# One score pair to a step: regrouping the scores of an attention stage

## The reference

```python
def block(args):
    qi, i = args
    s = jnp.einsum('bqhmd,bkhmd->bhmqk', qi, kf)
    q_chunk = (i * Q_BLOCK + jnp.arange(Q_BLOCK)) // CHUNK
    mask = k_chunk[None, :] <= q_chunk[:, None]
    p = jax.nn.softmax(jnp.where(mask, s, -1e30), axis=-1)
    a = p[:, :, 0] - lam * p[:, :, 1]
    return jnp.einsum('bhqk,bkhe->bqhe', a, vf)
...
ga, gb, gc = jnp.split(jax.nn.sigmoid(h @ gate_w[l] + gate_b[l]), N_BRANCHES, axis=-1)
```

## Time and profile before

| | before |
|---|---|
| median of 3 runs | 3073.64 us (3070.15 to 3075.08) |
| the profiled execution: its time, its span | 3070.15 us, 3068.3 us |
| TensorE busy over the span | 2786.3 us, 91% |
| VectorE busy | 1984.3 us, 65% |
| ScalarE busy | 1462.1 us, 48% |
| attention stage, from and to | 511 to 1166 us of the span |

### The profile page before, as it was taken

One profiled execution on the slowest core, in us unless ns is written; L12 is line 12 of the kernel. 1 busy time (PEld: TensorE's weight loads), 2 busy tenths in 40 slices (PEclk: granted clock), 3 DMA queues, 4 the chain that ended last, 5 costly groups with the idle time before them and its releaser, 6 DMA issues. The chain is left out here.

```text
span 3068.3 us, 41252 instructions
## 1 busy us (share of the span) xinstructions
PE 2786.3 (91%) x13492; PEld 2197.5 (72%) x13493; DVE 1984.3 (65%) x3104; ACT 1462.1 (48%) x2353; POOL 388.4 (13%) x289
## 2 busy tenths in 40 slices
PE   4999887989999997899996898995999999999996
PEld 3767665777777775788874677884777777777774
DVE  6657995555545465544453564437888888888874
ACT  4414553555556463323343333212666666666663
POOL 3101221000000001101110001110122222222211
PEclk9999999999999998989997999997999999999998
DMA  6275325131322226311127997533989997877875
GB/s 229 92 261 198 96 83 149 57 117 59 97 83 80 78 78 238 96 42 52 49 76 249 307 314 263 198 139 139 367 269 308 355 369 246 284 234 219 264 256 144
DMA packets 292202, 554.80 MB, mean 181 GB/s; under 512 B 32089, under 2 KB 98905, under 8 KB 288482
## 3 DMA queue, kind: packets, MB, share of 16 engines
q1 hardware_dynamic: 273666, 492.06, 46.3%
q0 software_dynamic: 14400, 52.44, 7.0%
q10 hardware_dynamic: 4000, 8.53, 0.9%
HBM read 418.21 MB, written 143.15 MB: 183 GB/s over the span
## 5 line engine op out<-in xcount | busy, mean ns | idle before, releaser
L2596 DVE TENSOR_TENSOR moe_w_lo<-moe_W,moe_w_hi 128x1024 fp32r<-128x1024 f32 x384 | 461.0, 1221 | 85.5 <-ACT moe_w_hi L2524 72.1
L2524 ACT CAST moe_w_hi<-moe_W 128x1024 fp32r (+1 forms) x384 | 401.3, 1052 | 152.2 <-PE moe_h1b L2447 77.1
L1562 PE MATMUL project_bank<-h_lo,w_hi 128*128 128x512 f32 x512 | 201.7, 394 | 0.0
L340 PE MATMUL att_bank<-h_hi,w_hi 128*128 128x512 f32 x384 | 169.6, 442 | 17.0 <-PEq L137 11.6
L2472 PE MATMUL moe_yb<-moe_W,moe_hT 128*128 x384 | 172.5, 592 | 0.0
L519 DVE TENSOR_SCALAR_CACHE_REDUCE att_S<-att_bank 128x512 f32<-128x512 f32 x192 | 122.3, 687 | 63.5 <-PE att_bank L307 63.5
L2445 PE MATMUL moe_h1b<-moe_w_hi,moe_xT_hi 128*128 128x512 f32 x384 | 156.4, 407 | 4.8 <-DVE moe_xT_lo L2607 4.8
L425 ACT ACTIVATE att_S<-att_S,att_nm 128x128 f32<-128x128 f32 (+15 forms) x128 | 154.0, 1205 | 7.5 <-DVE att_nm L527 7.5
L341 PE MATMUL att_bank<-h_lo,w_hi 128*128 128x512 f32 x384 | 152.0, 396 | 0.0
L342 PE MATMUL att_bank<-h_hi,w_lo 128*128 128x512 f32 x384 | 152.0, 396 | 0.0
L2447 PE MATMUL moe_h1b<-moe_w_hi,moe_xT_lo 128*128 128x512 f32 x384 | 151.7, 395 | 0.0
(11 more groups left out here) (478 smaller groups left out, 6929.8 us busy)
## 6 DMA issues: line engine op xcount, KB each, us to landing
moe_W<-in_moe_w SPq DMA_DIRECT2D x96, 2048.0 KB, 13.4
w_raw<-in_gate_w SPq DMA_DIRECT2D x48, 512.0 KB, 3.9
out_sg<-gateT SPq DMA_DIRECT2D x32, 768.0 KB, 11.1
gateT<-att_gates SPq DMA_DIRECT2D x48, 256.0 KB, 2.3
gateT<-gate_out SPq DMA_DIRECT2D x48, 256.0 KB, 2.4
early<-in_ada_w SPq DMA_DIRECT2D x8, 1024.0 KB, 9.3
project_spare<-in_x SPq DMA_DIRECT2D x16, 512.0 KB, 6.2
w_raw<-in_w_in SPq DMA_DIRECT2D x16, 512.0 KB, 4.4
```

What stands on the lines that cost most here:

```text
L340: pe.matmul(bank[7][:], w_hi[b][:, k, :], h_hi[:, k, at], start=k == 0, stop=False)
L1562: pe.matmul(bank[n % 4][:], w_hi[b][:, k, :], low[:, k, at512(tb)], start=False, stop=False)
L2524: nc.scalar.copy(w_hi[:, slot(p, first), :], raw(at, p)).then_inc(q["w13_high"], 1)
L2596: nc.vector.tensor_tensor(w_lo[:, own, :], raw(at, p), w_hi[:, own, :].bitcast(F32), ALU.subtract).then_inc(q["w1_low" if p < 4 else "w3_l ...
```

## The change

TensorE makes the scores of `ahead` spread over the steps that are left, rounding up: with 1 to 4 pairs and 2 to 5 steps this is one pair in each step from step 0 on, until they are used up. VectorE evacuates three quarters of `ahead`, rounded up, ahead of the scales and the weighing: 1, 2, 3 and 3 pairs of 1, 2, 3 and 4, where it was 1, 2, 2 and 2. For three pairs (tiles 6 to 9) none is left behind the weighing, for four (tiles 10 to 13) one. The number of instructions and their sizes stay.

```diff
-    def scored_in(step, ahead):
-
-        return ahead[step:step + 2] if step % 2 == 0 else []
...
-                            for p in scored_in(n - lo, ahead):
-                                score(h, p)
+                            for _ in range(-(-len(ahead) // (hi + 1 - n))):
+                                score(h, ahead.pop(0))
...
-                        for p in ahead[:2]:
+                        most = -(-len(ahead) * 3 // 4)
+                        for p in ahead[:most]:
                             evacuate(h, p)
                         scales(item + 1)
                         weigh(item + 1)
-                        for p in ahead[2:]:
+                        for p in ahead[most:]:
                             evacuate(h, p)
```

## The result

The changed kernel takes 3109.07 us (median of 4 runs, 3101.39 to 3116.32), the kernel before 3074.36 (4 runs). The ratio is 1.0102, with a 95% interval of 1.0084 to 1.012: slower by 1.0%. Over all 22 runs on record the changed kernel's median is 3106.73 us (3098.35 to 3116.32). The prediction was 3105 us, slower. The profiled execution took 3104.89 us with a span of 3103.1, 34.8 us more than before.

What follows compares the result with a forecast made beforehand. TensorE was taken to bound the attention stage. Group costs and later weighings, less vanished stalls, summed to 8.07 us a head, 32.3 in four, giving 3102.5 or 3106 us, stated as 3105; range 3084 to 3119.

Steps and rivals of the forecast that it cites:

- TensorE sets the pace: Attention stage, 655 us long: TensorE busy in 610.53 us, so added TensorE work and its waits count.
- a group costs s = 0.37 us: TensorE, each group of score matmuls: 0.37 us at its edges; 16 more groups a head, 5.9 us.
- the two halves I read: Edges of a score group: 0.20 us more for two singles than a double, 0.17 more for transposes followed by scores.
- Tiles 2, 4, 5 and 12: One more group's price each in tiles 2, 4, 5 (+0.37 us), two in tile 12 (+0.74).
- The third evacuation holds the weighing in tiles 6 to 9: VectorE's weighing waits for the third pair's late scores, delaying the next tile: +0.62, +0.69, +1.74, +1.85 us.
- the 0.54 us: Tile 6, TensorE's wait for the gate bank: credited as vanishing, 0.54 us, within that tile's +0.62.
- Tiles 3, 10, 11, 13: Later second pair, +1.0 us; later weighing, +0.57 and +0.75; two more groups less a 0.32 us stall, +0.42.
- The maxima of tile 15 come in time: Tile 14: exponentials of tile 15 start 1.42 us earlier, TensorE's 1.43 us stall shrinks by as much: -1.42 us.
- The sum: All tile terms of the attention stage together: 8.07 us a head, 32.3 us in four heads.
- some 24 us: Attention stage: growth of TensorE's busy time and gaps at the edges of score groups, 38 groups a head.
- The DMA queue: SP's loads of the next head's q and k, 2 to 3 us later in tile 13: costed at nothing.

Runs made afterwards that it cites:

- the split: Kernel before, one gate group of step 0 put between its two pairs of scores in tiles 2 to 13: 3086.77 us, ratio 1.0047.
- TensorE's part alone: Kernel before with one pair of scores in a step, VectorE still evacuating two pairs ahead of the weighing: 3088.61 us, ratio 1.005.
- gates first: Kernel before, step 0's gate group ahead of scores in tiles 6, 13; three of four pairs evacuated before weighing in 10, 13: 3058.62 us, ratio 0.9952.
- VectorE's part alone: Kernel before, three of three or four pairs evacuated ahead of the weighing, TensorE's scores left in their steps: 3086.45 us, ratio 1.0037.

## Why the prediction was right

**TensorE sets the pace, and a group costs s = 0.37 us.** Right. In the place of the split it is made up of other parts than the two halves I read; that both places come to nearly the same sum I had assumed and not worked out. Tiles 2, 4, 5 and 12 were to lose 0.37, 0.37, 0.37 and 0.74 and lost 0.35, 0.46, 0.37 and 0.85. The split in place measures 0.37 to 0.40. TensorE's part alone came to 15.3 us over the kernel before (3088.61 against 3073.35, the median of the runs beside it) where I expected 17.

**The third evacuation holds the weighing in tiles 6 to 9.** Right, and about half of the loss: put back, it gives 3.8 of the 7.35 us a head. +0.62, +0.69, +1.74, +1.85 forecast, +0.29, +0.55, +1.62, +1.85 measured. Tile 6 is the worst of the terms. I credited the 0.54 us that its row shows as a wait; a gate matmul that hasn't waited follows three transposes so much sooner that the stall was worth about 0.9 (TensorE's part alone: 9.22 to 8.65 although it pays 0.37; gates first: 1.02 with no group to pay). The time to take from a stall is that between two starts, less that between the same two without it, and not the bracket. Tile 6's +0.62 came out too high by that.

**Tiles 3, 10, 11, 13.** +1.0, +0.57, +0.75, +0.42 forecast, +0.85, +0.57, +0.63, +0.29 measured.

**The maxima of tile 15 come in time.** Right: -1.42 forecast, -1.32 measured.

**The sum.** 8.07 us a head forecast, 7.35 in the third head, 7.40 in the last. Of the 34.8 us of span, the tiles of the four heads hold 30.3. Another 0.6 stands ahead of the first tile, 1.7 between heads and 2.2 behind the start of the last tile; of these the forecast knew nothing, and that they made up for a sum that was 2 us too high is luck. The 2.2 can't be told from chance: from that start to the end of the span the kernels with the same later stages take between 1921.1 and 1932.6 us, whatever their edit, and the kernel before 1921.8. The 30.3 holds two disturbed spots that pull against each other. One is the clock in the changed kernel's second head, 1.5 us, below. The other stands in the first head of the kernel before, where tile 1 takes 8.21 us instead of 7.25 because ScalarE's copy of its transposes comes behind a gate weight that was loaded late:

```profile
538.35 1.05 ACT L410 CAST w_hi<-w_raw 128x1024 fp32r<-128x1024 f32 x1 [3.64 <-DMA w_raw<-in_gate_w]
```

TensorE's busy time in the stage was to grow by some 24 us and grew by 31.3. In the third head it grows by 6.6, of which TensorE's part alone makes 5.8 and VectorE's part alone 0.5.

**The DMA queue.** The later loads of q and k cost nothing that shows: the lengths from a head's tile 15 to the next head's first tile grow by 1.3, 0.3 and 0.1 us, and not by the same amount each time, as a late load would make them. TensorE waits for a load of q and k in the first head alone, in both kernels (0.9 and 1.2 us).

## What to carry to other kernels

Count how often TensorE changes between full-row and half-row matmuls, and not only the matmuls: here 64 more excursions cost some 24 us of TensorE by the measured price (15 us of time by themselves, since stalls take some of it up), about what the best kernel of this study gained by removing stalls, 15 us. An idle gap on an engine that isn't the bound can be filled only with work whose input is there before the gap ends; compare the moment at which the producer is done with the end of the gap, to the tenth of a microsecond, tile by tile. And when a mixed change has lost, cut it by tile: two of its effects were gains, and with a gate group moved ahead of the scores they made a kernel 0.5% faster than the one before.

## What I had not expected

A stall of TensorE sometimes costs twice. In the changed kernel's second head, tile 8 takes 11.01 us instead of 9.47 in the first and third. It starts with the same wait of 1.56 us for the weighing as in the others, but here the granted clock falls to half behind it (0.50 in the windows of 1 us from 766 to 769, the level of 1.2 GHz); windows across it, same columns as above:

```profile
755.00:762.00 7.00, 7.00 (x47) 5.36 (x44) 3.33 (x13) 3.78 (x7) 0.00 (x0) 1.00 0.36 109
762.00:766.00 4.00, 2.44 (x16) 1.56 (x15) 2.26 (x7) 2.11 (x5) 0.00 (x0) 0.95 0.02 7
766.00:770.00 4.00, 4.00 (x17) 2.58 (x16) 1.63 (x7) 2.48 (x5) 0.00 (x0) 0.62 0.00 0
```

```profile
765.39 0.65 PE L336 MATMUL att_bank<-h_hi,w_hi 128*128 128x512 f32 x1
765.84 0.63 PE L337 MATMUL att_bank<-h_lo,w_hi 128*128 128x512 f32 x1
766.27 0.63 PE L338 MATMUL att_bank<-h_hi,w_lo 128*128 128x512 f32 x1
766.69 1.05 PE L313 MATMUL att_bank<-consts,att_S 128*128 128x128 f32 x4
```

Gate matmuls then start 0.43 us apart instead of 0.23, and the tile loses 1.5 us. TensorE was busy in all of the 7 us up to 762 and in 2.44 of the 4 us that hold the stall. VectorE's part alone has the same spot in tile 8 of its last head (10.57 us instead of 9.05). It befell one of four such stalls in each of the two traces; what sets that one apart no run shows, nor whether longer stalls bring it about more often.
